# Attention's rotary step done by halves: q is finished, restacked and reloaded while k is still in work

## The reference

```python
def rope(x):
    ang = jnp.arange(S, dtype=f32)[:, None] * inv_freq[None, :]
    x1, x2 = x[..., : d // 2], x[..., d // 2:]
    return jnp.concatenate([x1 * cos - x2 * sin, x1 * sin + x2 * cos], axis=-1)
...
qa = rope(q_a.astype(f32).reshape(B, S, ATT_HEADS, ATT_HEAD_DIM))
ka = rope(k_a.astype(f32).reshape(B, S, ATT_HEADS, ATT_HEAD_DIM))
y_a = dilated_attention(qa, ka, va).reshape(B, S, ATT_WIDTH).astype(x.dtype)
```

## Time and profile before

| | us |
|---|---|
| median of 3 runs | 4135.39 (4134.15 to 4135.9) |
| the profiled execution, its own time | 4136.65 |
| its span in the trace | 4134.9 |
| TensorE busy | 3941.6 (95%) |
| GpSimd busy | 1693.8 (41%) |
| attention's tiles, pair 0 to pair 5 | 685.3 to 924.5 of the span |

### The profile page before, as it was taken

The page is one execution under the profiler, slowest core; times in us unless marked ns, Lnnn a source line. Parts: engine busy times, 40 slices in busy tenths (PEclk is TensorE's granted clock), DMA queues, the critical chain, the costliest instruction groups (busy, mean ns, idle before and its releaser), DMA issues. The chain is left out here.

```text
span 4134.9 us, 59363 instructions
## 1 busy us (share of the span) xinstructions
PE 3941.6 (95%) x21744; PEld 3556.9 (86%) x21744; DVE 2570.5 (62%) x5129; ACT 1377.0 (33%) x2227; POOL 1693.8 (41%) x1134
## 2 busy tenths in 40 slices
PE   8999999898998898999999999999989999999998
PEld 7888887787888778999999999999987888888887
DVE  1135213455555453148588878876648988899988
ACT  2234223552333211112653645626522222222221
POOL 0000022624444000004457566566636666666663
PEclk9999999899999999999999999999999999999999
DMA  3323343543222432234479698698888888888884
GB/s 109 101 94 120 127 132 109 140 104 113 79 79 95 164 104 82 81 124 110 117 231 292 211 291 263 203 345 261 269 290 306 308 296 297 307 294 317 312 295 183
DMA packets 390357, 801.62 MB, mean 194 GB/s; under 512 B 64944, under 2 KB 203696, under 8 KB 389168
## 3 DMA queue, kind: packets, MB, share of 16 engines
q1 hardware_dynamic: 279600, 530.95, 38.5%
q0 software_dynamic: 110592, 268.62, 21.0%
HBM read 623.15 MB, written 154.27 MB: 188 GB/s over the span
## 5 line engine op out<-in xcount | busy, mean ns | idle before, releaser
L2039 PE MATMUL r_psd<-x1h,r_dh 128*128 128x384 f32 x2048 | 700.8, 342 | 7.5 <-DVE r_dl L1837 7.4
L2039 PE MATMUL r_psd<-x1l,r_dh 128*128 128x384 f32 x2048 | 688.4, 336 | 0.0
L2039 PE MATMUL r_psd<-x1h,r_dl 128*128 128x384 f32 x2048 | 688.4, 336 | 0.0
L2301 PE MATMUL e_psy<-e_uh,e_Ch 128*128 128x512 f32 x1536 | 599.6, 390 | 15.2 <-DVE e_Cl L2220 15.2
L2301 PE MATMUL e_psy<-e_ul,e_Ch 128*128 128x512 f32 x1536 | 599.2, 390 | 0.0
L2301 PE MATMUL e_psy<-e_uh,e_Cl 128*128 128x512 f32 x1536 | 598.9, 390 | 0.0
L1812 POOL DMA_INDIRECT W<-r_put,r_place x256 | 429.5, 1678 | 395.9 <-DVEq L1986 303.0
L2258 DVE SCALAR_TENSOR_TENSOR e_y<-e_rows,coef,e_y 128x1024 f32<-128x1024 f32 x254 | 417.0, 1642 | 0.0
L2185 POOL DMA_INDIRECT e_rows<-in_up,ids x256 | 383.1, 1497 | 59.5 <-issue 51.1
L1803 POOL DMA_INDIRECT r_rows<-in_down_rows,ids x256 | 262.7, 1026 | 351.2 <-DVE coef L1854 240.4
L2039 PEld LDWEIGHTS r_psd<-x1h,r_dh 128*128 128x128 f32 x2048 | 388.3, 190 | 8.2 <-DVE r_dl L1837 8.2
(11 more groups left out here) (339 smaller groups left out, 7392.5 us busy)
## 6 DMA issues: line engine op xcount, KB each, us to landing
hand<-in_down SPq DMA_DIRECT2D x128, 512.0 KB, 5.4
hand<-in_up SPq DMA_DIRECT2D x128, 512.0 KB, 7.4
act<-r_act SPq DMA_DIRECT2D x128, 384.0 KB, 5.1
e_W<-W SPq DMA_DIRECT2D x128, 384.0 KB, 6.4
W<-r_W SPq DMA_DIRECT2D x32, 1024.0 KB, 12.9
p_wraw<-in_w_in SPq DMA_DIRECT2D x58, 512.0 KB, 4.4
hT<-p_out SPq DMA_DIRECT2D x58, 512.0 KB, 2.9
hand<-act SPq DMA_DIRECT2D x64, 384.0 KB, 5.2
```

What stands on the lines that cost most here:

```text
L2039: ins = nc.tensor.matmul(psd[n][:, h, 0:HD], a[c % DEEP][:, k, :], b[:, k, h * HD:(h + 1) * HD], start=(k == 0 and m == 0), stop=(k == KD ...
L2301: ins = nc.tensor.matmul(bank[:], a[s][:, t * P:(t + 1) * P], v[s][:, h * HALF:(h + 1) * HALF], start=(q == 0 and m == 0), stop=(q == G - ...
```

## The change

GpSimd, in every pair: the two products of q come first, then the wait for the previous restack, then q's sums and difference; k's two products, which stood ahead of that wait, come behind q's difference, and then k's sums and difference.

SyncE, for pairs 1 and 2 only: the first `ahead` is written out. When q of pair 1 is done (split at 3) it restacks q of pair 1 (four DMAs) and loads raw q of pair 2 (five DMAs); when k is done it loads raw k of pair 2 (five) and restacks k of pair 1 (eight). The number of DMAs is the same. From the second `ahead` on SyncE's order is as before.

```diff
-            def load(i):
-                for n, first in ((0, 0), (2, AT)):
+            def load(i, pair=None):
+                for n, first in ((0, 0), (2, AT)) if pair is None else ((2 * pair, AT * pair),):
...
-            def restack(par):
+            def restack(par, pair=None):
                 for h in range(HPT):
                     rows = slice(h * AD, (h + 1) * AD)
                     for n, parts in enumerate(((qk_hi[0], qk_lo[0]), (qk_hi[1], qk_hi[1]), (qk_lo[1], qk_lo[1]))):
+                        if pair is not None and min(n, 1) != pair:
+                            continue
...
-            with sp.Fori(0, AT // 2 - 1) as j:
+            sp.wait_ge(split, START + 3)
+            restack(1, 0)
+            load(2, 0)
+            sp.wait_ge(split, START + 4)
+            load(2, 1)
+            restack(1, 1)
+            sp.wait_ge(pv_done, START + ITEMS)
+            columns(2, 0)
+            ahead(0, 1)
+            with sp.Fori(1, AT // 2 - 1) as j:
                 ahead(j, 0)
                 ahead(j, 1)
...
-                for n in range(4):
-                    multiply(nc.gpsimd, pool, i, n)
-                pool.wait_ge(stacked[u], START + use)
                 for n in range(2):
+                    multiply(nc.gpsimd, pool, i, 2 * n)
+                    multiply(nc.gpsimd, pool, i, 2 * n + 1)
+                    if n == 0:
+                        pool.wait_ge(stacked[u], START + use)
                     add_and_split(nc.gpsimd, pool, n, 4 * i + (2 * n + 2), 4 * i + (2 * n + 2))
```

## The result

The changed kernel takes 4145.17 us (median of 16 runs, 4138.56 to 4151.32) where the kernel before takes 4135.84 (16 runs, 4132.26 to 4144.0). The ratio is 1.0021, with a 95% interval from 1.0013 to 1.0029: 8.7 us slower, between 5.4 and 12. The forecast of 4140.7 us is a ratio of 1.0013, the lower end of that interval, and the median stands 0.2 us above the range that was given. Its profiled execution took 4149.62 us, with a span of 4147.8.

A forecast was written before the change was run, and what follows sets the result against it. GpSimd's rope and SyncE's load and restack were taken to set pair starts: 9.0 us gained at pair 1, 4.75 lost each later turn, pair 5 +5.3. 4135.39 + 5.3 = 4140.7 us, range 4133.5 to 4145.

The forecast's parts named there:

- The ring of rope, load and restack: Attention: GpSimd's sums, then SyncE's load and restack, 38.7 us a turn on the mean, set when pairs 2 and 4 start.
- The start gives 9.0 us: Pair 1 starts 9.0 us earlier (8.4 to 9.4): four restacks fewer 4.8, half a load less 4.3, minus 0.1.
- The early part: q's four restacks and half load on SyncE's queue: out by about 710, before k is done at 711.3.
- Each later turn costs 4.75 us: GpSimd's ropes of pairs 2 to 5: k's two products no longer hidden, its part grows from 14.3 to 19.05 us.
- Pair 4 at +5.3: Pair 4's stacks come 5.3 us later (+4.9 to +5.9); pair 5 then starts 5.3 later (+4.1 to +6.2).
- The size of "same": Whole kernel: a measurement can tell about 0.2% (8.3 us) from no change; same was given 84 in 100.
- The clock: TensorE's clock falls to half where it waited, tile behind takes 35.4 to 38.4 us; longer waits cost no more.
- the lower bound for tile 4: TensorE's tile of pair 4: at shortest 35.4 us, the shortest tile that followed a wait; 37.5 taken.
- products stay hidden: Rival: GpSimd's turns don't lengthen, all pairs keep the 9.0 us; 4126.5 us, 0.22% faster; 4 in 100.
- half of it is hidden: Rival: load or restack runs faster, a turn grows by only 2 to 3.5 us; 4132 to 4137 us; 10 in 100.
- The start gives less: Rival: q's load still queued when k is done, start gives 4.8 instead of 9.0; 4144.9 us; 10 in 100.
- The shift is swallowed behind attention: Rival: attention's delay doesn't reach the stages behind it; 4135.4 us; 5 in 100.

The follow-up runs named there:

- the repeat: The changed kernel timed and traced once more, nothing altered, against the kernel before: 4144.4 us, ratio 1.0024.
- one_product_moved: The changed kernel, but in ropes 2 to 5 only k's second product stands behind the wait; against the kernel before: 4135.98 us, ratio 1.0000.
- pool_order_only: Only GpSimd's new order, SyncE as before, against the kernel before: 4150.79 us, ratio 1.0038.
- start_only: SyncE as in the change, rope 1 by halves, GpSimd's ropes 2 to 5 in the old order; against the kernel before: 4130.36 us, ratio 0.9983.
- halves_all_old_pool: SyncE restacks and loads by halves in every turn, first rope by halves, GpSimd's later ropes in old order; against the kernel before: 4121.36 us, ratio 0.9967.
- act_unrolled: SyncE by halves in every turn, GpSimd's later ropes in old order, ScalarE's pair loop written out; against the kernel before: 4117.26 us, ratio 0.9947.

## Why the prediction was right in its steps, and short in its sum

- **The ring of rope, load and restack sets the starts of the pairs: shown.** Lengthening a turn, shortening the start, half a dose and writing out ScalarE's loop each moved the starts as the ring says, and once SyncE went by halves in every turn, the waits after pair 1 were gone.
- **The start gives 9.0 us: it gave 8.6** in the changed kernel's trace, 9.2 in its repeat, 10.0 in the start alone and 8.0 in one_product_moved, the same start again. The restacks' part was forecast at 4.8 and measured at 5.0. The early part did not collide with k's; in the trace of after SyncE had issued it by 708.90, and k's load went out at 713.62.
- **Each later turn costs 4.75 us: the three turns cost 14.06 together** (42.93, 42.91 and 44.25, against 39.12, 38.35 and 38.56), where 14.25 was forecast. GpSimd's part is as computed, 19.04 against 19.05; single turns differ by 1.3 us through the transfers. In pool_order_only the three cost 13.2, in the repeat 16.1.
- **Pair 4 at +5.3: +5.45, and +6.9 in the repeat.** In the profiled execution of after the tile of pair 4 was the longest of the bounds given (38.3 us, PEclk 0.88), which makes pair 5 +6.3 and not +5.3: the term of the sum that was mis-sized is this tile, for which I took 37.5. In the repeat that tile took 37.6, and the mis-sized term is the turns, 16.1 us where I took 14.25: pair 5 comes at +7.05. GpSimd's part of a turn was 19.03 there as well, so it is load and restack that took longer; why they did is open.
- **The rest of the difference is not settled.** Attention accounts for 6.3 to 7.1 us of 8.7 (5.4 to 12). The missing 2 us are inside the interval. The last stage came out at another size in the repeat, and the way to DeltaNet has the length of after in seven other kernels, one of them the kernel before but for ScalarE's loop. Over all eleven comparisons of this study the measured time stands 2 to 5 us above the shift of pair 5 in seven, and within 0.4 us of it in four. Every shift is counted from one single trace of before: if attention in that execution was 2 us longer than usual, it would look so. No second trace of before was taken, so this stays a guess.
- **The size of "same" was too small a picture.** It rested on three runs of before that lay within 1.75 us. Sixteen runs spread over 11.7 us, and one measurement of 16 against 16 has an interval of 6.6 us. The forecast +5.3 and the measured +8.7 can hardly be told apart by it. The repeat's interval (1.0014 to 1.0035) lies just above the forecast's 1.0013, so the forecast is more likely a little too low than right, as attention's own +6.3 and +7.05 say.
- **The clock.** I read the longer tiles of pairs 2 and 4 as the price of the waits ahead of them, and from pair 1's shorter tile I concluded that a longer wait doesn't cost more. That compared an odd tile with even ones. Sorted by what stands at their start, the tiles of pairs 1 to 4 of all twelve traces are:

| tile starts with | us | PEclk | tiles |
|---|---|---|---|
| neither wait nor table load | 34.3 to 34.9 | 1.00 | 10 |
| a wait of 0.7 us | 34.4 | 1.00 | 1 |
| a wait of 1.2 to 11.6 us | 35.3 to 36.8 | 0.91 to 0.95 | 19 |
| the table load | 37.5 to 37.6 | 0.95 | 4 |
| the table load and a wait of 2.3 to 8.6 us | 37.4 to 38.4 | 0.88 to 0.91 | 14 |

Compared within odd and within even tiles, a wait alone costs 0.4 to 2.4 us in the tile, the table load alone 2.7, and a wait on top of the table load -0.2 to 0.8. Within the third row the length doesn't follow the wait (35.4 behind 1.24 us and 35.4 behind 11.3), so that much of the step holds, as does its remark that a slow start varies: tile 4 of the changed kernel took 38.3 in one execution and 37.6 in the other, behind waits of 8.0 and 8.6. What failed is the lower bound for tile 4: 35.4 was an odd tile's, and no tile with the table load took less than 37.4. The forecast's own value, 37.5, was near that end. The wrong reading did no more harm to the sum, but it hid 5.7 us that were to be had.

Of the rivals, "products stay hidden" and "half of it is hidden" fell with pool_order_only (+13.6 us at pair 5). "The start gives less" fell with the start's 8.6 us; the time it would have given, 4144.9, is the one that was measured, for another reason, and that agreement is chance. "The shift is swallowed behind attention" fell too: in start_only, pool_order_only and halves_all_old_pool pair 5 moved by -10.2, +13.6 and -16.1 us, and the time by -7.0, +15.7 and -13.6.

## What to carry to other kernels

When an operation is moved from ahead of a wait to behind it, ask what the wait was hiding: here two products lay under 9 us of waiting, and the change took them out in every turn to gain once at the start. Splitting work by halves pays where the consumer goes by halves too; GpSimd's new order cost 14 us with the old SyncE order and nothing with the new one. And before a long tile is put down to the wait ahead of it, compare it with a tile of the same instructions that had no such wait.

## What was not expected of the hardware

- An activation table load of 1.28 us on ScalarE at the start of each loop body made a tile 2.8 us longer, since TensorE ran dry and its granted clock fell. The windows of TensorE at the start of tile 2 in halves_all_old_pool (length, busy, PEclk, DMA share, GB/s):

```profile
766.00:768.00 2.00, 1.13 (x6) 1.00 0.30 92
768.00:770.00 2.00, 0.60 (x3) 0.94 0.58 174
770.00:772.00 2.00, 2.00 (x8) 0.50 0.08 16
772.00:774.00 2.00, 2.00 (x12) 0.70 1.00 201
```

TensorE was idle for only 2.3 of 4 us, in two pieces (0.84 us for VectorE, 1.43 for ScalarE), and the granted clock was 0.50 in the next 2 us. In act_unrolled, without the load, the first piece is there and the second is not, and the clock stayed at 1.00 over the same place.

- The way from attention to DeltaNet took one of two lengths in the twelve traces, 14.5 us (three) or 15.8 to 15.9 (nine), and nothing between. None of the edits sorts them; whether it is chance of the execution or belongs to the built kernel isn't shown, since the one kernel traced twice gave 15.8 both times.
